# Banded attention with a softmax sink: a column for the sink in each head's row, the negated maximum straight from VectorE, and two pieces of work in other places of their engines' orders

## The reference, cut to what matters

```python
def sink_softmax(scores, sink):
    sink_b = jnp.broadcast_to(sink, scores.shape[:-1] + (1,))
    p = jax.nn.softmax(jnp.concatenate([scores, sink_b], axis=-1), axis=-1)
    return p[..., :-1]
...
    wmask = in_band[None] & ((blk > 0) | (jj[None] >= SWA_BLOCK))
    s_win = jnp.where(wmask[None, :, None, None], s_win, -jnp.inf)
    p = sink_softmax(jnp.concatenate([s_meta, s_win], axis=-1),
                     sink[None, None, :, :, None, None]).astype(dtype)
    orr = (jnp.einsum('bnkgqj,bjkd->bnqkgd', p[..., :N_META], vm)
           + jnp.einsum('bnkgqj,bnjkd->bnqkgd', p[..., N_META:], vw))
```

## Time and profile before

| | us |
|---|---|
| median of 3 runs | 2627.0 |
| lowest and highest of them | 2622.95, 2630.43 |
| the profiled execution, its own time | 2619.92 |
| its span in the trace | 2618.3 |
| the banded attention in it, about 1551 to 1642 | about 91 |

### The profile page before, as it was taken

The page is one execution under the profiler, slowest core; times in us unless marked ns, Lnnn a source line. Parts: engine busy times, 40 slices in busy tenths (PEclk is TensorE's granted clock), DMA queues, the critical chain, the costliest instruction groups (busy, mean ns, idle before and its releaser), DMA issues.

```text
span 2618.3 us, 31423 instructions
## 1 busy us (share of the span) xinstructions
PE 2499.8 (95%) x12220; PEld 2031.6 (78%) x12220; DVE 1594.5 (61%) x2074; ACT 1078.1 (41%) x1748; POOL 215.4 (8%) x353
## 2 busy tenths in 40 slices
PE   6999999999889999998999998999998999999997
PEld 5777888888667777877888775897787888888886
DVE  7666566555665665466652547036737777687779
ACT  6444322333565656222421325133525444443333
POOL 0001111111000000100010002100001112110000
PEclk9999999999999999999999988999999999999999
DMA  4222333334021121634133310111042444584432
GB/s 139 89 96 89 106 108 107 108 104 170 28 77 66 50 76 48 237 103 178 36 100 127 121 33 1 49 33 33 17 135 105 157 142 157 174 304 146 161 131 108
DMA packets 138011, 278.36 MB, mean 106 GB/s; under 512 B 16653, under 2 KB 91066, under 8 KB 130074
## 3 DMA queue, kind: packets, MB, share of 16 engines
q1 hardware_dynamic: 108202, 176.52, 20.3%
q0 software_dynamic: 29680, 100.07, 10.8%
HBM read 196.86 MB, written 79.69 MB: 106 GB/s over the span
## 4 chain that ended last, share of the span: by engine, by line
PE 81%; DVE 7%; ACT 5%; DVEq 2%; issue 2%; ACTq 1%; DMA 1%; SPq 0%; POOL 0%; POOLq 0%
PE ps L2571 32%; PE ps L585 12%; PE ps L3203 10%; PE ps L2815 6%; PE ps L2665 3%; PE ps L2649 2%; PE ps L579 2%; PE ps L2622 2%; PE ps L3097 1%; PE ps L2879 1%; DVEq L1926 1%; PE ps L2579 1%; PE ps L2633 1%; PE ps L2800 1%; PE ps L3082 1%
## 5 line engine op out<-in xcount | busy, mean ns | idle before, releaser
L1849 DVE TENSOR_TENSOR proj_out<-ps,proj_out 128x512 f32<-128x512 f32 x292 | 195.9, 686 | 255.6 <-PE ps L2571 250.6
L2571 PE MATMUL ps<-a_hi,pw_hi 128*128 128x512 f32 x528 | 213.5, 404 | 0.8 <-ACT proj_out L1222 0.8
L2571 PE MATMUL ps<-a_lo,pw_hi 128*128 128x512 f32 x528 | 205.8, 390 | 0.0
L2571 PE MATMUL ps<-t_hi,pw_hi 128*128 128x512 f32 x464 | 188.7, 407 | 0.0
L2571 PE MATMUL ps<-t_lo,pw_hi 128*128 128x512 f32 x464 | 180.9, 390 | 0.0
L2571 PE MATMUL ps<-a_hi,pw_lo 128*128 128x512 f32 x352 | 137.5, 391 | 0.0
L565 DVE TENSOR_TENSOR w_lo<-w_raw,w_hi 128x2048 fp32r<-128x2048 f32 x28 | 64.0, 2287 | 115.4 <-ACT w_hi L561 110.1
L1919 DVE TENSOR_TENSOR_SCAN c<-l,r 128x128 f32<-128x128 f32 (+7 forms) x64 | 86.7, 1355 | 58.1 <-ACT l L1336 57.7
L561 ACT ACTIVATE w_hi<-w_raw 128x2048 fp32r<-128x2048 f32 x28 | 53.6, 1914 | 164.0 <-DMA w_raw<-in_w_out 64.6
L2571 PEld LDWEIGHTS ps<-a_hi,pw_hi 128*128 128x128 f32 x528 | 99.2, 188 | 24.8 <-issue 5.0
L2571 PEld LDWEIGHTS ps<-a_lo,pw_hi 128*128 128x128 f32 x528 | 99.2, 188 | 23.6 <-issue 3.8
(11 more groups left out here) (490 smaller groups left out, 6666.2 us busy)
## 6 DMA issues: line engine op xcount, KB each, us to landing
pw_raw<-in_w_in SPq DMA_DIRECT2D x30, 1024.0 KB, 6.0
hidden_raw<-hidden_forms SPq DMA_DIRECT2D x28, 1024.0 KB, 4.8
projections<-proj_out POOLq DMA_DIRECT2D x88, 256.0 KB, 3.4
w_raw<-in_w_in SPq DMA_DIRECT2D x18, 1024.0 KB, 5.3
pw_raw<-in_w_ff SPq DMA_DIRECT2D x16, 1024.0 KB, 5.9
w_quarter<-in_w_ff SPq DMA_DIRECT2D x16, 1024.0 KB, 7.4
hidden_forms<-proj_out POOLq DMA_DIRECT2D x56, 256.0 KB, 3.6
hidden_forms<-nb POOLq DMA_DIRECT2D x56, 256.0 KB, 3.5
```

The lines of the kernel that those rows point to most:

```text
L1849: return dve.tensor_tensor(out_ap(n, j), product_bank(n, o), src, ALU.add)
L2571: last = pe.matmul(product_bank(n, o), w, a[:, k0 + k, t], start=(k == 0 and g == 0), stop=(k == 3 and g == 2))
```

## The change

- The row of each head gets a column for its sink: band 128, meta 16, sink, sink, meta 16, band 128. The two heads of a pair keep their data side by side; `LEADS` is 34, the middle part with both sinks, in place of 32. ACT writes the two by two sink logits of a step (`sink_columns`) in front of each copy of the own scores, before it waits for the scores.
- The maximum of L2165 then covers the sink, and with `negate=True` it is put out negated. L2169, L2171 and L2172 go, with two drains.
- The exponentials run over 145 columns, their row sums hold the sink term, and the separate exponential of it (L1530) and the sum (L2178) go. The product with the reciprocal covers 145 columns a head.
- The sink's probability is transposed along with the meta columns. The rows of the meta values `SVM` that it meets are zero (34 rows in place of 32), so it adds nothing.
- ACT's order: own(2) is put in front of exp(1), and in each step the copy of the own scores, now of E+3, comes behind the turned copies of E and in front of exp(E+2).
- PE's order: in each step out(E-1) comes in front of turn(E).

```diff
--- before.py
+++ after.py
@@ -14,6 +14,8 @@
 SB_HEADS, RET_HEADS = 8, 4
 GLA_LEVELS = (64, 32, 16, 8, 4, 2, 1, 0)
 KEYS = P + META
+LEADS = 2 * META + 2
+PAIR = 2 * P + LEADS
 NEG = -1.0e30
 LOG_EXP = "natural_log_exp_and_others"
 CLAMP = 40.0
@@ -172,7 +174,7 @@
     SQ = work("sq", [P, 4, SEQ])
     SK = work("sk", [P, NT])
     SV = work("sv", [P, TT, P])
-    SVM = work("svm", [2 * META, P])
+    SVM = work("svm", [LEADS, P])
     VD = work("value_steps", [P, TT - 1, P])
     pos[0] = work_at + 36 * KB
     pcos = work("pcos", [P, NT])
@@ -183,7 +185,7 @@
     KMR = work("kmr", [P, META])
     window = work("window", [P, 3, P])
     sinks = work("sinks", [P, 8])
-    SS = [work(f"ss{u}", [P, 2, 2 * KEYS + 2 * META]) for u in range(3)]
+    SS = [work(f"ss{u}", [P, 2, P + LEADS + P + LEADS]) for u in range(3)]
     PR = [work(f"pr{u}", [P, HALF]) for u in range(2)]
     SM = work("sm", [P, 3, 4, 4])
     PT = [[at(f"pt{u}{c}", [P, HALF], off=out_at + (3 * u + c) * HALF * 4) for c in range(3)] for u in range(2)]
@@ -512,7 +514,15 @@
 
         def probs(E):
 
-            return SS[E % 3][:, :, 0:2 * KEYS].rearrange("p a (b c) -> p a b c", b=2)
+            return SS[E % 3][:, :, 0:PAIR].rearrange("p a (b c) -> p a b c", b=2)
+
+        def own_and_meta(E):
+
+            return SS[E % 3][:, :, 0:2 * (KEYS + 2)].rearrange("p a (b c) -> p a b c", b=2)[:, :, :, 0:KEYS]
+
+        def sink_columns(E):
+
+            return SS[E % 3][:, :, KEYS:KEYS + 2]
 
         def band(E):
 
@@ -1088,7 +1098,7 @@
             pool.wait_ge(n2.lo, TT + 1)
             pool.memset(SVM[:, :], 0.0).then_inc(sv_zero, 1)
             pool.wait_ge(sv_ok, 1)
-            pool.dma_start(SVM[META:2 * META, 64:P], KMV[:, :]).then_inc(tables_in, 16)
+            pool.dma_start(SVM[META + 2:LEADS, 64:P], KMV[:, :]).then_inc(tables_in, 16)
             pool.wait_ge(sv_ok, 3)
             pool.tensor_tensor(VD[:, :, :], SV[:, 0:TT - 1, :], SV[:, 1:TT, :], ALU.subtract).then_inc(sv_ok, 1)
             pool.wait_ge(tables_in, 16 * 5)
@@ -1517,31 +1527,36 @@
                 act.activation(SV[:, 4 * h:4 * h + 4, :], bank[6 + h].rearrange("p (t c) -> p t c", t=4), ACT.Copy).then_inc(sv_ok, 1)
             def window_own(E):
 
-                act.wait_ge(s_done, E + 1)
+                if E == 0:
+                    act.wait_ge(tables_in, 16 * 5)
                 if E >= 3:
                     act.wait_ge(t_done, E - 2)
-                act.activation(probs(E), ps[:, 0:4, P:P + KEYS].rearrange("p (a b) c -> p a b c", b=2), ACT.Copy).then_inc(sk_ok, 1)
+                e = E % 2
+                act.activation(sink_columns(E), sinks[:, :].rearrange("p (g i) -> p i g", g=2)[:, 2 * e:2 * e + 2, :], ACT.Copy)
+                act.wait_ge(s_done, E + 1)
+                act.activation(own_and_meta(E), ps[:, 0:4, P:P + KEYS].rearrange("p (a b) c -> p a b c", b=2), ACT.Copy).then_inc(sk_ok, 1)
 
             def window_exp(E):
                 act.wait_ge(s_max, E + 1)
                 for h in range(4):
-                    z = SS[E % 3][:, h // 2, (h % 2) * KEYS:(h % 2 + 1) * KEYS]
-                    act.activation(z, z, ACT.Exp, bias=SM[:, E % 3, 0, h:h + 1], accum_out=SM[:, E % 3, 1, h:h + 1])
-                act.activation(SM[:, E % 3, 2, :], SM[:, E % 3, 2, :], ACT.Exp).then_inc(s_exp, 1)
+                    z = SS[E % 3][:, h // 2, (h % 2) * (KEYS + 1):(h % 2 + 1) * (KEYS + 1)]
+                    last = act.activation(z, z, ACT.Exp, bias=SM[:, E % 3, 0, h:h + 1], accum_out=SM[:, E % 3, 1, h:h + 1])
+                last.then_inc(s_exp, 1)
 
             def window_keep_turned(E):
                 act.wait_ge(t_done, E + 1)
                 act.activation(PT[E % 2][0][:, :], bank[4 + E % 2], ACT.Copy)
-                act.activation(PT[E % 2][2][0:2 * META, 0:2 * P], bank[6][0:2 * META, 0:2 * P], ACT.Copy).then_inc(pt_a, 1)
+                act.activation(PT[E % 2][2][0:LEADS, 0:2 * P], bank[6][0:LEADS, 0:2 * P], ACT.Copy).then_inc(pt_a, 1)
 
             window_own(0)
             window_own(1)
             window_exp(0)
+            window_own(2)
             window_exp(1)
             for E in range(16):
-                if E < 14:
-                    window_own(E + 2)
                 window_keep_turned(E)
+                if E < 13:
+                    window_own(E + 3)
                 if E < 14:
                     window_exp(E + 2)
 
@@ -2162,24 +2177,15 @@
                     other = window[:, 1, :].unsqueeze(1).unsqueeze(1).broadcast_to([P, 2, 2, P])
                 dve.copy_predicated(band(E), mask, other).then_inc(s_copied, 1)
                 dve.wait_ge(s_copied, E + 1)
-                dve.tensor_reduce(SM[:, u, 0, :].rearrange("p (a b) -> p a b", b=2), probs(E), AX.X, ALU.max)
-                dve.drain()
-                sink = sinks[:, :].rearrange("p (g i) -> p i g", g=2)[:, 2 * g:2 * g + 2, :]
-                top, rest = (SM[:, u, c, :].rearrange("p (a b) -> p a b", b=2) for c in (0, 2))
-                dve.tensor_tensor(top, top, sink, ALU.max)
-                dve.drain()
-                dve.tensor_tensor(rest, sink, top, ALU.subtract)
-                dve.tensor_scalar(SM[:, u, 0, :], SM[:, u, 0, :], -1.0, None, ALU.mult)
+                dve.tensor_reduce(SM[:, u, 0, :].rearrange("p (a b) -> p a b", b=2), probs(E), AX.X, ALU.max, negate=True)
                 dve.drain().then_inc(s_max, 1)
 
             def window_back(E):
                 u = E % 3
                 dve.wait_ge(s_exp, E + 1)
-                dve.tensor_tensor(SM[:, u, 3, :], SM[:, u, 1, :], SM[:, u, 2, :], ALU.add)
+                dve.reciprocal(SM[:, u, 3, :], SM[:, u, 1, :])
                 dve.drain()
-                dve.reciprocal(SM[:, u, 3, :], SM[:, u, 3, :])
-                dve.drain()
-                dve.tensor_tensor(probs(E), probs(E), SM[:, u, 3, :].rearrange("p (a b) -> p a b", b=2).unsqueeze(3).broadcast_to([P, 2, 2, KEYS]),
+                dve.tensor_tensor(probs(E), probs(E), SM[:, u, 3, :].rearrange("p (a b) -> p a b", b=2).unsqueeze(3).broadcast_to([P, 2, 2, KEYS + 1]),
                                   ALU.mult).then_inc(p_ready, 1)
 
             def window_keep_out(E):
@@ -2979,10 +2985,10 @@
                     pe.wait_ge(pt_a, E)
                 for h in range(4):
                     at_ = ((h % 2) * 2 + h // 2) * P
-                    lo = (h % 2) * (P + 2 * META)
+                    lo = (h % 2) * (P + LEADS)
                     pe.transpose(bank[4 + E % 2][:, at_:at_ + P], SS[u][:, h // 2, lo:lo + P], ident[:, :])
                 for i in range(2):
-                    last = pe.transpose(bank[6][0:2 * META, i * P:(i + 1) * P], SS[u][:, i, P:P + 2 * META], ident[:, :])
+                    last = pe.transpose(bank[6][0:LEADS, i * P:(i + 1) * P], SS[u][:, i, P:P + LEADS], ident[:, :])
                 last.then_inc(t_done, 1)
 
             def window_out(E):
@@ -2997,7 +3003,7 @@
                     pe.wait_ge(so_kept, E)
                 c0, c1 = slice(0, 2 * P), slice(2 * P, 4 * P)
                 o0, o1 = bank[7][0:64, 0:2 * P], bank[7][64:P, 0:2 * P]
-                pe.matmul(bank[7][:, 0:2 * P], SVM[:, :], PT[u][2][0:2 * META, 0:2 * P], start=True, stop=False)
+                pe.matmul(bank[7][:, 0:2 * P], SVM[:, :], PT[u][2][0:LEADS, 0:2 * P], start=True, stop=False)
                 pe.matmul(o0, SV[:, n, 0:64], PT[u][0][:, c0], start=False, stop=(n == 0))
                 last = pe.matmul(o1, SV[:, n, 64:P], PT[u][0][:, c1], start=False, stop=(n == 0))
                 if n:
@@ -3011,9 +3017,9 @@
             for E in range(16):
                 if E < 14:
                     window_scores(E + 2)
-                window_turn(E)
                 if E >= 1:
                     window_out(E - 1)
+                window_turn(E)
             window_out(15)
 
 
```

## The result

The changed kernel takes 2609.97 us (median of 6 runs, 2606.86 to 2614.77) against 2625.92 (6 runs, 2619.29 to 2630.94). The ratio is 0.9948, interval 0.9932 to 0.9964: faster by 9 to 18 us, some 16 by the medians. The prediction was 2620.7 with a range of 2614 to 2628, so the gain is two and a half times the forecast of 6.3 us, and the time lies outside the range. The profiled execution took 2606.86 us, 13.1 less than that of before.

A forecast was written before the change was run, and what follows sets the result against it. Bound: PE at low clock, a 4.86 us ACT-DVE ring at full clock. New end 1585.75 + 1.64 + 11 x 4.0 + 4.50 = 1635.9 against 1642.17, gain 6.3 us; from median 2627.0 that gives 2620.7, range 2614 to 2628.

The forecast's parts named there:

- the ring between ACT and DVE: Full-clock steps before: exponentials, own-score copy, predicated copy, maximum and small operations in series, 4.86 us a step.
- a forecast of 4.0: Period of one step at full clock after the change: 4.0 us, between 3.9 and 4.3, in place of 4.86.
- The ring that PE's new order closes: Turn(E), turned copies, POOL's masked copy, out(E), then turn(E+1): 3.91 us, equal to PE's own work.
- The 34 columns and rows, the sink copy and the 145th column: Added work per step: taken as 0, at most 0.1 us for the transposes; 145th column under 0.01 us per instruction.
- Rival (b): Each step, DVE's product (L2182) starts behind POOL's copy and waits: p 4.3 to 4.8, 2624 to 2629.5; chance 0.14.
- Rival (d): ACT's moved copy still waits, now for PE's scores, and no ring was opened: 2625 to 2628; chance 0.03.
- Up to 1585.75 PE is full in both versions, so it has done the same work there: Low-clock first part: same work done by 1585.75, then 1.64 us for out(3) and eleven steps of 4.0 us.
- Rival (a): Clock returns elsewhere or earlier, each 3 us sooner saving about 1.5: gain 8 to 10 us, 2617 to 2619; chance 0.28.
- 7.1 us under the median: Profiled execution 2619.92 against median 2627.0; the 6.3 us gain was taken off both, giving 2613.6 and 2620.7.
- the ring of rows 4 is open: ACT's order: own(E+3) in front of exp(E+2), so the copy no longer waits for exponentials; 4.86 us ring opened.
- The slower rival (c): Clock stays at 1.2 GHz to the stage's end, steps up to 7.8 us: net 35 us slower, 2662; chance 0.05.

The follow-up runs named there:

- e_before_stepfill: Kernel before plus one unused PE product of 128x256 in front of turn(E), E = 2 to 13: 2619.96 us against 2625.49, ratio 0.9984.
- e_before_fill: Kernel before plus five unused PE products of 128x512, four behind scores(0), one behind scores(1): 2625.98 us, ratio 0.9994.

## Why the prediction was wrong

**What held.** At full clock the bound passed from the ring between ACT and DVE to PE, and the step came out at 3.93 us for a forecast of 4.0 (bounds 3.9 to 4.3). The ring that PE's new order closes is there, 2.1 us of waits for POOL, and at the end the two last turns lost what the old order had. The 34 columns and rows, the sink copy and the 145th column cost nothing that shows. Rival (b) didn't happen in the changed kernel: the product always began first and stayed at 0.762 to 0.765 us, and POOL's copy, behind it, took 1.27 us and once 1.36. It did happen with ACT's order alone. Rival (d) is out by the step of 3.93.

**The step that failed** is the sentence on which the sum rests: "Up to 1585.75 PE is full in both versions, so it has done the same work there", with eleven steps at full clock behind it. It took the end of the low clock from one execution as a fixed point. In the changed kernel the low time in the first 55 us was 18 and 10 us in place of 31. Redone from the rows of the first profiled execution, the sum comes out like this:

| part of the stage | predicted us | measured us |
|---|---|---|
| first scores to turn 4 | 36.2 | 30.1 |
| turn 4 to turn 13, nine steps | 36.0 | 35.4 |
| turn 13 to turn 15 | 8.0 | 9.4 |
| turn 15 to the next product | 4.5 | 4.35 |
| sum | 84.7 | 79.2 |

The miss in the stage is in the first row, 6.1 us; the last turns gave 1.4 of it back. What a shorter low stretch is worth, runs of the kernel before tell: over 28 of them 0.001 of mean clock goes with 2.0 us, and 0.001 of 2625 us is 5.25 us at low clock, so 0.38 us for each. The steps say the same: one takes 6.37 us at low clock, as before, and 3.93 at full, and 1 - 3.93/6.37 is 0.38. For 13 us less at low clock that makes 5.0 of the 6.1 (an estimate); the other 1.1 I can't place. Rival (a) was the right case, with a size too small: I priced one or two pieces of 3 us and a gain of 8 to 10.

**The second part of it** is the base. I noted that the profiled execution stood 7.1 us under the median and carried that over as a constant. It wasn't one: the changed kernel's stood 3.1 under its median, which is 4.0 of the miss of 10.7 us; 5.5 are the stage and some 1.3 lie between the two profiled executions outside it. The clock goes with this: the runs of the kernel before average a clock of 0.9797, some 107 us low; the profiled one had 0.982, or 94. The changed kernel averages 0.9823, 92 us, its profiled one 0.983. The kernel before so spends some 14 us more at low clock over its runs (11 to 19 by the batch), about 5.5 us of the gain by the slope; the other 10 or so are there at equal clock. That is an estimate, and it agrees with the 11 us of the two versions with products without use. Both profiled executions were better than most: that of before is 6 us under the median of all six runs, that of after 3.

**Where the prediction misread the change.** It began with the order on ACT ("the ring of rows 4 is open") and gave no split between the parts. The sink's column alone brings the step to 3.9 to 4.0 and all of the gain (2606.32); ACT's order alone stops at 4.35 to 4.74, with the product held up by POOL. PE's 3.9 is the floor; with the column in, ACT's order takes the last 0.07 us off a step, nothing that the times can tell. PE's order costs 2.4 us at equal clock.

**The slower rival (c)**, a clock that stays low, is what PE's order alone showed in pieces: waits in the steps, then 0.66 and 0.50 in a stretch long after the start. In the changed kernel PE has no such waits before the last two steps.

**Open** is why the low stretch is shorter. It is in every version whose steps wait less (10 to 27 us in nine profiled executions of the changed kernel, of it with PE's old order, with and without the move on POOL, and of the column or ACT's order alone; 31 in all three of the kernel before, 24 and 27 in it with products without use; 40 with PE's order alone). No single part decides it: without PE's order, with the column alone and with ACT's order alone it was 10 us in one execution and 24 or more in the other. That fewer waits of PE shorten it fits all of this and e_before_stepfill, but was not shown by itself; in the low stretch steps took 6.4 us in the kernel before and in the changed one, and from 1570 to 1580 PE was busy 10.00 of 10 us in the first.

## What to carry to other kernels

Where two engines pass a step to and fro, shorten the longer side first and look at which engine is the floor; a reordering that opens the ring may be worth nothing after that, and one on the floor engine can close a new ring. Before a low stretch of the clock is used as a fixed point of a sum, look at the clocks of all runs: if the profiled execution differs from the median by more than the effect, the spread is part of the price. Waits of PE inside a stage may cost twice, once as waits and once as clock: with PE's order alone both came together. And where an edit moves an operation of DVE with two SBUF inputs, look at what POOL does just then: with ACT's order alone the product was held up by 0.7 to 0.9 us in each step.

## What the runs showed of the hardware

The low clock did not end when PE's records were full again: in the kernel before PE was busy 10.00 of 10 us from 1570 to 1580 at 0.50, and the low stretch lasted 31 us in three executions. Nor did it take a standstill of 3 us: with the idle start filled (e_before_fill), the clock fell behind the stretch in which PE was busy 3.36 of 5 us, where its longest wait was 1.2 us. A product without use on PE can pay for itself: with them the changed kernel went from 2609.97 to 2604.07 us.

Operations of DVE and POOL that both read two SBUF tensors hold each other up, and the later one pays. The rotation sum took 2.42 us beside POOL's differences and 0.69 without. With ACT's order alone the product began behind POOL's copy and took 1.67 for 0.76. With PE's old order in the changed kernel (e_no_pe_order) it is the other way round, and POOL's copy pays, 1.42 for 1.27:

```profile
1586.11 0.77 DVE L2188 TENSOR_TENSOR ss<-ss,sm 128x580 f32<-128x580 f32 x1
...
1586.58 1.42 POOL L1107 TENSOR_TENSOR pt<-pt,window 128x512 f32<-128x512 f32 x1 [2.45 <-ACT pt L1549]
```

How much is paid is regular. In all eighteen traces of this case, wherever POOL's masked copy met such an operation of DVE and the two records overlapped by more than 0.16 us (156 times), the later one was longer than alone by the overlap less 0.13 to 0.16 us; where they overlapped by 0.16 us or less (52 times), neither was longer by more than 0.02. In the rows above the overlap is 0.30 and the copy 0.15 longer. The Trainium skill, "SBUF — State Buffer", section "Who interferes with whom", has such a pair exclude each other for the whole instruction. The traces agree but for the last 0.15 us of the record that began first, which cost the other nothing here.
